# Moving eight channel products and eight convolutions of the second half from the first half's attention to behind the first expert choice

## The reference, cut to what matters

```python
proj = rmsnorm(x) @ w_in                       # z, xbc, dt, q, k, v
xbc = silu(causal_depthwise_conv(xbc, conv_w, conv_b))   # 4 taps along the tokens, 1024 channels
y_ssd = ssd(z, xbc, dt)                        # chunk scan, 8 heads
y_diff = softmax(q1 k1) v - lam * softmax(q2 k2) v       # 4 heads, chunk-causal
x = x + concat(y_ssd, y_diff) @ w_out
q = rmsnorm(x) @ w_q                           # 8 heads x 2 halves x 128
idx, g = top 16 of the 16 x 16 sums of the top 16 of each half's 128 key scores
h = gelu(x . u[idx])                           # 128 expert rows of u for each token
x = x + sum(softmax(g) * h * v[idx])           # and of v
```

## Time and profile before

| what | value |
|---|---|
| median of 3 runs | 1382.42 us |
| the profiled execution's own time | 1382.48 us |
| its span, first to last instruction | 1380.7 us |
| PE busy | 1344.0 us, 97% of the span |
| DVE busy | 1070.0 us, 77% |
| ACT busy | 434.3 us, 31% |
| mean DMA rate | 345 GB/s |
| mean granted clock of PE | 0.991 |

### The profile page before, as it was taken

One profiled execution on the slowest core, in us unless ns is written; L12 is line 12 of the kernel. 1 busy time (PEld: TensorE's weight loads), 2 busy tenths in 40 slices (PEclk: granted clock), 3 DMA queues, 4 the chain that ended last, 5 costly groups with the idle time before them and its releaser, 6 DMA issues.

```text
span 1380.7 us, 16366 instructions
## 1 busy us (share of the span) xinstructions
PE 1344.0 (97%) x5450; PEld 941.1 (68%) x5450; DVE 1070.0 (77%) x2415; ACT 434.3 (31%) x1220; POOL 608.5 (44%) x532
## 2 busy tenths in 40 slices
PE   8999999999999999999999999999999999999993
PEld 6656648567588999999999999974444444444441
DVE  4635445799899999999998999988677667765667
ACT  2633532444412121113787887750000000000000
POOL 0000001632856653382555555645657544544541
PEclk9999999999999999999999999999999999999997
DMA  8432234985999999999899999999999999999997
GB/s 318 158 112 93 117 143 180 365 302 199 403 396 411 409 407 391 349 398 389 334 405 391 398 385 397 385 379 367 411 409 410 409 409 409 410 409 409 409 409 311
DMA packets 123923, 476.20 MB, mean 345 GB/s; under 512 B 13888, under 2 KB 14400, under 8 KB 117312
## 3 DMA queue, kind: packets, MB, share of 16 engines
q0 software_dynamic: 76032, 276.86, 51.1%
q1 hardware_dynamic: 47520, 197.78, 36.7%
q10 hardware_dynamic: 288, 0.52, 0.1%
HBM read 471.17 MB, written 3.93 MB: 344 GB/s over the span
## 4 chain that ended last, share of the span: by engine, by line
PE 47%; DVE 23%; DMA 20%; issue 5%; POOL 2%; ACT 2%; DVEq 0%; SPq 0%; ACTq 0%; POOLq 0%
PE BANKS L999 14%; PE BANKS L797 11%; DMA BIG<-u,IDX 11%; DMA BIG<-v,IDX 9%; PE BANKS L1039 8%; DVE X L1775 7%; PE BANKS L789 6%; PE BANKS L1034 4%; DVE BIG L1770 2%; DVE BIG L1536 1%; DVE BIG L1532 1%; DVE BIG L1539 1%; POOL BIG L1825 1%; DVE UV L1770 1%; DVE BIG L1606 1%
## 5 line engine op out<-in xcount | busy, mean ns | idle before, releaser
L1825 POOL DMA_INDIRECT UV<-u,IDX x150 | 172.4, 1150 | 406.6 <-DVE IDX L1613 258.3
L1825 POOL DMA_INDIRECT UV<-v,IDX x157 | 180.9, 1152 | 143.6 <-DVE UV L1770 69.2
L1775 DVE SCALAR_TENSOR_TENSOR X<-UV,HG,X 128x1024 f32<-128x1024 f32 x157 | 201.1, 1281 | 38.0 <-DMA UV<-v,IDX 36.2
L1039 PE MATMUL BANKS<-T,BIG 128*128 128x512 f32 x512 | 225.2, 592 | 0.0
L1039 PE MATMUL BANKS<-Y,BIG 128*128 128x512 f32 x512 | 225.1, 592 | 0.0
L999 PE MATMUL BANKS<-T 128*128 128x240 f32 x1024 | 215.6, 366 | 0.3 <-DMA T<-u_t 0.3
L1770 DVE SCALAR_TENSOR_TENSOR UV<-UV,Y 128x1024 f32<-128x1024 f32 x150 | 182.8, 1222 | 40.4 <-DMA UV<-u,IDX 39.8
L999 PE MATMUL BANKS<-T,Y 128*128 128x240 f32 x992 | 209.0, 366 | 0.0
L999 PEld LDWEIGHTS BANKS<-T 128*128 128x128 f32 x1024 | 192.0, 190 | 12.6 <-DMA T<-u_t 0.6
L999 PEld LDWEIGHTS BANKS<-T,Y 128*128 128x128 f32 x992 | 185.8, 190 | 11.5
L1039 PEld LDWEIGHTS BANKS<-Y,BIG 128*128 128x128 f32 x512 | 97.3, 190 | 122.5 <-issue 122.2
(11 more groups left out here) (284 smaller groups left out, 1277.8 us busy)
## 6 DMA issues: line engine op xcount, KB each, us to landing
T<-u_t SPq DMA_DIRECT2D x64, 512.0 KB, 6.8
T<-v SPq DMA_DIRECT2D x64, 512.0 KB, 6.8
Y<-v SPq DMA_DIRECT2D x64, 512.0 KB, 6.8
Y<-u_t SPq DMA_DIRECT2D x62, 512.0 KB, 6.8
BIG<-w_in SPq DMA_DIRECT2D x23, 1024.0 KB, 6.9
BIG<-w_q SPq DMA_DIRECT2D x16, 1024.0 KB, 7.7
BIG<-w_out SPq DMA_DIRECT2D x8, 1024.0 KB, 6.8
UV<-v,IDX POOLq DMA_INDIRECT x157, 8.7
```

The source lines that it names most:

```text
L1039: return nc.tensor.matmul(PS[6 - 2 * t + n][:, :], HBUF[:, j, t * P:(t + 1) * P], STREAM[j % NS][:, n * HALF:(n + 1) * HALF], start=(j == ...
L1775: stt(xb, row, HG[:, n % 2, i % UNIT:i % UNIT + 1], xb, ALU.mult, ALU.add).then_inc(used, 1)
L1825: pool.indirect_dma_start(row_place(s), None, v if kind == "rv" else u, bass.IndirectOffsetOnAxis(at, 0)).then_inc(row_in[k], 16)
```

## The change: the moved steps

The eight products, the eight convolutions and the weight tiles that the products need come later; ten rows are put among the convolutions, and the rows of three later attention steps are counted anew (step 8: 3 to 1, step 13: 1 to 2, step 14: 3 to 4). The first two row places in `XBC` open only after the last convolution, so the count at which they open is raised by the rows ahead of it. No instruction is added or removed. Lines in the changed kernel are 2 higher from here on.

```diff
-    after = {i: many("x", 9 + i, min(10 + i, 16)) for i in range(8)}
-    after[4] += on("T", 0)
-    after[7] += on("N n2", 1) + on("R0", 0) + on("T", 1) + many("cv", 8, 10) + on("R1 Q", 0) + many("cv", 10, 12)
-    after[7] += on("R0", 1) + many("cv", 12, 14) + on("F", 0) + on("R1 Q", 1) + on("U", 0) + on("F", 1) + on("k", 2)
+    after = {4: on("T", 0)}
+    after[7] = on("N n2", 1) + on("R0", 0) + on("T", 1) + on("R1 Q", 0)
+    after[7] += on("R0", 1) + on("F", 0) + on("R1 Q", 1) + on("U", 0) + on("F", 1) + on("k", 2)
     after[7] += on("U", 1) + on("k", 3)
-    o += attention(0, 8, after, on("x", 8))
+    o += attention(0, 8, after, [])
...
-    o += many("cv", 14, 16) + many("W", 0, 4) + many("K", 0, 2) + on("ks k1", 1) + many("W", 4, 8) + many("K", 2, 4)
-    o += whole(0) + on("z", 2) + on("D", 2) + on("k2", 1) + on("S1", 2) + on("z", 3) + many("qt", 4, 6) + rows(3) + on("M", 2) + rows(6)
+    o += many("W", 0, 4) + many("K", 0, 2) + on("ks k1", 1) + whole(0) + many("x", 8, 11)
+    for i in range(11, 16):
+        o += on("x", i) + on("cv", i - 3) + rows(1 + i % 2)
+    o += many("W", 4, 6) + on("cv", 13) + rows(1) + many("W", 6, 7) + on("cv", 14) + rows(1) + many("W", 7, 8) + on("cv", 15) + many("K", 2, 4)
+    o += on("z", 2) + on("D", 2) + on("k2", 1) + on("S1", 2) + on("z", 3) + many("qt", 4, 6) + rows(3) + on("M", 2) + rows(6)
...
-        after[i] = many("W", i + 1, min(i + 2, 16)) + (between[i]() if i in between else rows({8: 3, 13: 1, 14: 3, 15: 0}[i]))
+        after[i] = many("W", i + 1, min(i + 2, 16)) + (between[i]() if i in between else rows({8: 1, 13: 2, 14: 4, 15: 0}[i]))
...
-                first = RING + at // DM if name == "XBC" else rows_until(step) + in_use[name] + 1
+                first = rows_until(step) + RING + at // DM if name == "XBC" else rows_until(step) + in_use[name] + 1
...
-        tiles = in_x + zqkv + in_x + wo + [zqkv[2]] + wq[0:2] + [zqkv[0], zqkv[1], zqkv[3]] + wq[2:4] + wo + wq
+        tiles = in_x + zqkv + wo + [zqkv[2]] + wq[0:1] + in_x + wq[1:2] + [zqkv[0], zqkv[1], zqkv[3]] + wq[2:4] + wo + wq
```

More of the change, by code:

```diff
@@ L587, in block_program @@
         wq = [w_q[i] for i in range(4)]
-        tiles = in_x + zqkv + in_x + wo + [zqkv[2]] + wq[0:2] + [zqkv[0], zqkv[1], zqkv[3]] + wq[2:4] + wo + wq
+        tiles = in_x + zqkv + wo + [zqkv[2]] + wq[0:1] + in_x + wq[1:2] + [zqkv[0], zqkv[1], zqkv[3]] + wq[2:4] + wo + wq
         products_of = ([(proj_full, drained("x", 3)), (proj_full, drained("x", 7))]
                        + [(proj_full, drained(n, 1)) for n in "zqkv"]
-                       + [(fill_full, 4), (fill_full, 8), (res_full, RES[("R0", 1)] + 1), (res_full, RES[("R1", 1)] + 1), (proj_full, drained("k", 3))]
-                       + [(q2_full, 4), (q2_full, 8)] + [(proj_full, drained(n, 3)) for n in "zqv"]
+                       + [(res_full, RES[("R0", 1)] + 1), (res_full, RES[("R1", 1)] + 1), (proj_full, drained("k", 3))]
+                       + [(q2_full, 4), (fill_full, 4), (fill_full, 8), (q2_full, 8)] + [(proj_full, drained(n, 3)) for n in "zqv"]
                        + [(q2_full, 12), (q2_full, 16)]
@@ L634, in _ @@
                     sp.dma_start(KEYS_A, keys_t[:, PH:2 * PH, :]).then_inc(ld_keys, 16)
-                if n == 8:
+                if n == 6:
                     sp.wait_ge(y_free, 6)
```

## The result

The changed kernel takes 1406.49 us (median of 4 runs, 1404.31 to 1408.24) against 1382.03 of the kernel before (4 runs, 1379.86 to 1383.82): a ratio of 1.0173, 95% interval 1.0155 to 1.0191. The forecast was 1394, range 1377 to 1402: the direction was right, the size was missed by 12 us. The profiled execution took 1407.30 us, its span 1405.5.

What follows compares the result with a forecast made beforehand. The prediction took PE's order of work as the bound, with the rows' later end behind it. PE's end +27.7 us (-13.0 - 0.4 + 27.7 + 5.1 + 0.8 + 2.4 + 5.1) and tail -16.0 gave +11.7 on 1382.48: 1394 us, range 1377 to 1402.

Steps and rivals of the forecast that it cites:

- attention 1 and projections, to `W` 0: First half's attention 13.0 us shorter, PE's 0.40 us pause at `U` 0 gone, 1.7 us added for the clock.
- eight products: Behind the first choice, where PE is full: eight products at 3.46 us add 27.7 us.
- the 0.8: Behind the first choice: two smaller PE waits, 0.3 and 0.5 us, at `W` 5 and `K` 2.
- tail: Time from PE's last product to the span's end: some 5.2 us instead of 21.2, so -16.0.
- Rows of attention 2: Two rows fewer in step 8 bring nothing; one more on either side of the last head costs PE 2.4 us.
- 13.0 us earlier: Start of the first output projection, near 145.2 instead of 158.19; bounds 16 us and 11.
- the rival for the whole attention: The clock stays low in all of the first half's attention: 8.5 us more, 1402 us; chance 0.09.
- the two strands: PE's order of work and the first half's later-ending rows; moving rows forward can shorten only the second.
- the pause of 5.1: PE pauses 5.1 us ahead of `x` 15, awaiting ACT's copy behind a Silu, as the first gathers land late.
- The first rival: The rows are the bound and PE has slack: 1369 us, range 1366 to 1378; chance 0.16.
- the fall of the clock: Behind the existing 2.09 us pause at 376 to 380: low clock cost 1.7 us; no change forecast there.
- sign of being wrong that the prediction named: PE's last product moving by less than 12 us, or the rows still ending the span.

Runs made afterwards that it cites:

- e1_no_rows: The changed kernel without its ten rows between the convolutions, rows of attention 2 counted as before (3, 1, 3): 1404.76 us, ratio 1.0152.
- e15_first_indices: The changed kernel with the second choice's 32 first-pass rows fetched at the first choice's indices: 1399.44 us, ratio 1.0110.
- e10_both_filled: e7_both with matmuls that nothing reads added in PE's idle time of attention 1: 1392.81 us, ratio 1.0079.
- e4_copies_first: The changed kernel with the last five x products put ahead of the convolutions in the order, DVE's order the same: 1407.36 us, ratio 1.0195.
- e6_convs_ahead: The changed kernel with the ten rows behind the second to seventh convolution instead of the first to seventh: 1401.57 us, ratio 1.0154.
- e7_both: The changed kernel with the edits of e5_choice_earlier and e6_convs_ahead together: 1395.88 us, ratio 1.0096.
- e16_all_first_indices: e10_both_filled with the second choice's 32 first-pass rows fetched at the first choice's indices: 1387.22 us, ratio 1.0029.
- e5_choice_earlier: The changed kernel with the second choice one head earlier in attention 2 and the rows of steps 8 and 12 in step 12: 1403.64 us, ratio 1.0154.
- e2_rows_later: The changed kernel with five rows of steps 12 to 14 of attention 2 put behind the last transposes (U 3): 1412.80 us, ratio 1.0229.

## Why the prediction was wrong, step by step

| PE's shift, us | forecast | measured | what the runs showed |
|---|---|---|---|
| attention 1 and projections, to `W` 0 | -13.0 - 0.4 + 1.7 | -7.0 | the clock stays low in nearly all of attention 1: 3.6 to 4.1; the path itself 2.6 longer |
| eight products | +27.7 | +27.5 | as forecast (e1_no_rows) |
| pause ahead of `x` 15, clock, to `S1` 2 | +5.1 + 0.8 + 1.7 | +5.0 + 1.9 | as forecast; the 0.8 didn't come |
| attention 2, clock, to the products behind `U` | +2.4 + 1.7 | +7.8 | the first choice's rows run out |
| clock behind the pause at `U` | 0 | -1.7 | the pause stays, the clock doesn't fall |
| one-hots, to the end | 0 | +7.3 | the same cause, paid again by DVE: the pause of 3.76, and 3.1 at the low clock behind it |
| sum at PE's end | +27.7 | +40.8 | |
| tail | -16.0 | -16.0 | as forecast |

**The step that failed** is "Rows of attention 2 ... two rows fewer in step 8 bring nothing ... +2.4". It counted rows by DVE's time in each head and never by what they read. A row can be moved forward only as far as indices exist: with ten rows more, the 32 of the first choice end where the second choice is made, not some eight rows later. Taking that wait away gives back 7.1 us (e15_first_indices), in two places, at attention 2 and some 340 us further at the one-hots. In the profiled execution of that run `S1` 2 came 1.2 us later than in the changed kernel, and the clock fell behind the pause at `U`, which cost 1.7; by my estimate the wait is worth some 10 us (7.3 + 1.2 + 1.7) of the 11.0 by which these two stages exceed the forecast (7.8 - 4.1 + 7.3). The 2.4 itself was about right: without the wait the third projection is 2.3 us later against `S1` 2 than before (371.89 - 270.63 = 101.3 for 99.0).

**The attention was mis-sized.** "13.0 us earlier" became 7.3, outside the bounds of 11 to 16. With PE kept busy it took 30.1 us where 27.5 were forecast, so 2.6 of the error is the path; 0.6 is a later start of the first scores, and 2.5 is the clock up to the projection. I gave the clock 1.7 in the sum, for one pause, and 0.09 as the chance of the rival for the whole attention. That rival is what happened (a granted clock of 0.51 from 122 to 140 us and 0.50 from 140 to 151, where the kernel before has 1.00), but its price of 8.5 was too high: e10_both_filled gives back 4.1 at `S1` 2. Much of a head's path is on ACT and DVE, whose instructions took the same at either clock (for the wider heads an exponential 0.47 us, the weights 0.48, in the changed kernel as in e10_both_filled). The Trainium skill, "TensorE: Matmul & The Clock Gate", Part 1: The HAM clock gate, says that the default state is the throttled one and activity releases it; by that rule a thinly filled attention should lose the clock, and the traces agree: over the two windows it was 0.75 and 0.81 in the changed kernel, and 0.95 and 1.00 with the waits filled in e10_both_filled.

**What was right**: the two strands; the products' price; the pause of 5.1 and its cause in the first gathers (e4_copies_first and e6_convs_ahead bear it out); the tail, to 0.1 us. The first rival, slack on PE, is refuted by e1_no_rows: 20.4 us stay 20.4 us from `S1` 2 to the one-hots. Luck was the 1.7 us at `U`: the forecast kept the fall of the clock there, and in this execution it didn't happen; the miss would have been larger with it. Neither sign of being wrong that the prediction named came, as both looked for too small a loss.

**What stays open.** In e1_no_rows, e7_both and e16_all_first_indices PE's end is 4 to 5 us later than its third one-hot accounts for, with small waits spread between 690 and 950; in the changed kernel the 3.2 us behind its third one-hot are there at the fourth already (a granted clock of 0.64 from 703 to 712), and almost nothing is lost later. No run tells why.

## What to carry to other kernels

Before a consumer is moved forward, count what it consumes: indices, places in a ring, lead of the transfers. Where the supply comes in batches, find the item at which a batch runs out, before and after the move; the wait shows up there, and once more wherever the lost lead was needed. Where two engines are full side by side, a gain counts only if both get it: follow each strand's own marks (here DVE's indices and one-hots), not just the waits of the engine that ends last.

## What the runs showed of the hardware that was not expected

- In the emptied attention TensorE stood at the 1.2 GHz level for most of the stage (a granted clock of 0.51 from 122 to 140 us and 0.50 from 140 to 151), behind a wait of 2.40 us ahead of the first transpose and with single waits of 1.0 to 1.4 us between the heads after it, not just behind its one long wait. With 52 matmuls that nothing reads the clock stood at 0.95 and 1.00 over the two windows and `S1` 2 came 4.1 us earlier (e10_both_filled against e7_both); the time was 3.1 us less, with intervals that overlap.
- The same pause of 2.07 to 2.09 us ahead of the products behind `U` lowered the clock in some executions (four products in 15.74 us: before, e1_no_rows, e5_choice_earlier, e7_both, e15_first_indices) and not in others (14.05: changed, e2_rows_later, e4_copies_first, e6_convs_ahead, e10_both_filled, e16_all_first_indices). Its length alone doesn't tell.
- The DMA engines did not make up for gathers that were held back for 51 us: behind the gap they stand at a share of 1.02, as they do in the kernel before at that place (1.02 from 375 to 400 us in both), and DVE finds rows late 60 us after the indices came.
